# Token-tile start of the first projection, later squares for the second norm, and a PSUM bank for each late half-unit of w_out

## The chip, the cores and the metric

The kernel runs on one core of a Trainium2 chip. The metric is the device time of one launch in microseconds (us). Five engines work side by side, each through its own instruction queue in order: PE (TensorE, matrix products into the eight PSUM banks), DVE (VectorE), ACT (ScalarE), POOL (GpSimd) and SP (SyncE, which issues all the DMAs here). They wait for each other by semaphores alone.

## The reference, cut to what matters

Two layers run over 512 prompt tokens and 64 sample tokens, 576 in all, with a model width of 1024:

```python
for l in range(DEPTH):                       # DEPTH = 2
    xn = rmsnorm(x, norm_mix[l])             # over the 1024 columns of a token
    q, k, v, qi, ki, wi, u, gv = project(xn, w_in[l], pos)
    a = dsa(q, qi, wi, k, v, ki)             # indexer, top-k, attention
    bmix = gelu(u) * spatial(rmsnorm(gelu(gv), gate_norm[l]), w_spatial[l], b_spatial[l])
    x = x + concatenate([a, bmix]) @ w_out[l]
    h = relu(rmsnorm(x, norm_ffn[l]) @ w_ff1[l])
    x = x + (h * h) @ w_ff2[l]               # 1024 -> 4096 -> 1024
y = rmsnorm(x, norm_final)
```

Here `rmsnorm(x, g) = x * rsqrt(mean(x*x) + 1e-6) * g`.

## The kernel before

**Storage.** `x` is kept transposed: 8 column blocks j of 128 features, each over the 576 tokens. Products are made in three parts from float32r pairs: an operand is split into a high part (a rounded copy, made by ACT) and a low part (the rest, made by DVE). `xh` and `xl` are the two parts of x times the norm's gain. The factor 1/rms of a token isn't in them; it is applied later, to a product's result. Weights come in slots of 512 KB: SP loads a slot into one of two raw buffers, ACT writes `ring_hi` (`split_hi`, L631), DVE writes `ring_lo` (`split_lo`, L835), and four such pairs make a ring. A raw buffer is loaded again only when its `split_lo` is done.

**Start of layer 0.** SP issues four small DMAs of norm gains, then x in five token tiles (four of 128 rows and the sample's 64) with two weight slots between them. PE transposes each tile (L1163); ACT copies the blocks into `x` (L650). When all five tiles are there, ACT makes `xh` (L663) and a square (L645) column block by column block, DVE makes `xl` (`feed`, L840), and POOL adds the squares up into `ssacc` (`sum_squares`, L516 and L519). The first projection, QI (index queries), runs weight half by weight half over all tiles: 5 tiles x 2 halves x 12 matmuls of 256 columns (L1179). `row_sums` (L1151) sums `ssacc` over the partitions on PE, `row_mean` and a Newton step make 1/rms. Then PE does the narrow projection of the indexer's keys, `small` (L1373, 32 matmuls), whose weights DVE splits only behind `row_mean`.

**Order.** The rest of a layer up to its feed-forward part runs by ticks: lists written out by hand (`PE_AT`, `ACT_AT`, `DVE_AT`, `POOL_AT`) say what each engine does at each tick of PE's projection and w_out work.

**From w_out to the feed-forward part.** w_out is done in `NWO` = 32 half-units of 12 matmuls with 288 columns (L1211), each a column block j and half of the tokens. The last `KT` = 8, w = 24 to 31, finish blocks 0 to 7. All half-units alternate between banks 0 and 1, and half-unit w waits for the addition of half-unit w-2 (`wo_added`). DVE adds each into `x` (`wo_add`, L1040). When a late one is added, its block is complete, and ACT makes `xh` (L642) and the square (L645) of it, DVE `xl`, POOL adds the square; after every second block a slot of w_ff1 is split. PE's first feed-forward unit, u = 0, waits for all 32 additions and then, block by block, for `xl`. A unit is 48 matmuls of 288 columns into two banks (L1422); there are 64 a layer. Behind u = 1, PE sums `ssacc` into banks 0 and 1 (L1428), from which DVE makes `r2b`, the second norm's factor, used from u = 8 on.

Of the kernel before, what the change touches and what calls it, by code (L numbers as in the profile page):

```python
# [6 lines left out]
def hybrid_encoder_program(nc, A, O):  # L7
# [59 lines left out]
    UNITS = 2 * KT * GROUPS  # L67
    SLOTS = S_FFN + 2 * KT * GROUPS
# [20 lines left out]
    NWO = len(WOUT)  # L89

# [106 lines left out]
    with ctx:  # L197
# [80 lines left out]
        with ExitStack() as area:  # L278
# [3 lines left out]
            early = Area("early", TOK + NT * NSM + ID + P + 2 * NT * NR * 2 * RI + 2 * NT * NIH * ID)  # L282
            small_fm, zs2 = early.take(TOK), early.take(NT, NSM)
            cache_ki, grow = early.take(ID), early.take(P)[0:7 * KT]
            ra, rb = early.take(NT, NR * 2 * RI), early.take(NT, NR * 2 * RI)

            zq = early.take(NT, 2 * NIH * ID)
            early.used -= 2 * NT * NIH * ID
            rl = early.take(2, 2, SEQ)
            early.used = 0  # L290
# [31 lines left out]
        xT_done, xT_evac = sem("xT_done"), sem("xT_evac")  # L322
        gT_done, g_ready = sem("gT_done"), sem("g_ready")
# [28 lines left out]

        FIN_BANKS = [0, 1, 2, 3, 4, 6, 7]
# [29 lines left out]
        def _(sp):  # L383
            row = 0
# [6 lines left out]
            def load_x(t):  # L391
                src = A["x_prompt"][0, t * P:(t + 1) * P, :] if t < NPT else A["x_sample"][0]
                sp.dma_start(x_in[0:ROWS[t], t, :], src).then_inc(x_in_ready[t], 16)

            load_x(0)
            load_x(1)
            for l in range(DEPTH):
# [9 lines left out]
                for c, c0 in enumerate(CHUNKS):  # L407
                    for h in range(2):
                        load(A["w_in"][l, h * KH * P:(h + 1) * KH * P, c0:c0 + CW]
                             .rearrange("(k p) n -> p k n", p=P), KH)  # L410
                        if n[0] == 1:
                            for t in range(2, NT):
                                load_x(t)
# [80 lines left out]
        def _(pool):  # L494
# [13 lines left out]
            g.memset(ssv[:, :], 1.0).then_inc(const_made, 1)  # L508
            link(g.memset(mask0[:, :], 0.0))
# [44 lines left out]
            sum_squares(0)  # L554
            for l in range(DEPTH):
# [52 lines left out]
                for tick in range(G_LAST):  # L608
                    for kind, i in POOL_AT.get(tick, ()):
                        if kind == "gate_newton":  # L610
                            gate_newton(i)
                        elif kind == "gate":
                            gate(i)
                        else:
                            q_rope(i)
                sum_squares(KT * (2 * l + 1))
                sum_squares(KT * (2 * l + 2))
# [6 lines left out]
        def _(act):  # L624
# [8 lines left out]
            def feed(j, stage):  # L633
                base = KT * stage
                if stage % 2:
                    act.wait_ge(wo_added, NWO * (stage // 2 + 1) - KT + j + 1)
                elif stage:
                    act.wait_ge(x_ready, KT * (GROUPS * (stage // 2) - 1) + j + 1)
                else:
                    act.wait_ge(xT_evac, 2 * NT)  # L640
                if 0 < stage < 2 * DEPTH:
                    s.activation(xh[:, j, :], x[:, j, :], ACT.Copy, scale=gain(stage, j)).then_inc(xh_ready, 1)  # L642
                if base + j >= 2:
                    act.wait_ge(ss_added, base + j - 1)
                s.activation(sq[:, j % 2, :], x[:, j, :], ACT.Square).then_inc(sq_ready, 1)  # L645

            for t in range(NT):
                for half in range(2):
                    act.wait_ge(xT_done, 2 * t + half + 1)
                    s.activation(x[:, 4 * half:4 * half + 4, cols(t)],  # L650
                                 bank[2 * (t % 2) + half][:, 0:4 * ROWS[t]].rearrange("p (k n) -> p k n", k=4),
                                 ACT.Copy).then_inc(xT_evac, 1)
                if t == 1:
                    split_hi(0)

            act.wait_ge(g_ready, 1)
            for n in range(NSLOT):
                if n:
                    split_hi(n)
                if n == 0:  # L660
                    act.wait_ge(xT_evac, 2 * NT)
                for j in (2 * n, 2 * n + 1):
                    s.activation(xh[:, j, :], x[:, j, :], ACT.Copy, scale=gain(0, j)).then_inc(xh_ready, 1)  # L663
                for j in (2 * n, 2 * n + 1):
                    feed(j, 0)
            for l in range(DEPTH):
# [131 lines left out]
                for u in range(UNITS):  # L798
                    g, f = divmod(u, 2 * KT)
                    if f < KT:  # L800
# [8 lines left out]
                        s.activation(vh[:, f % KT, :], rl2[:, f % 2, :], ACT.Square).then_inc(h_high, 1)  # L809
                    elif g == GROUPS - 1:  # L810
# [671 lines left out]
```

## Time and profile before

| what | value |
|---|---|
| time, median of 3 runs | 1390.18 us (1389.63 to 1391.34) |
| the profiled execution: its own time | 1390.84 us |
| the profiled execution: span, first to last instruction | 1389.0 us |
| PE busy | 1336.8 us, 96% of the span |
| DVE, ACT, POOL busy | 54%, 37%, 9% |
| DMA | mean 74 GB/s, 16 engines 25% busy |

PE is the engine to read: the other engines idle about half of the time or more, and their idle time alone costs nothing. The places that matter are those at which PE has nothing to do. They show in the view of waits (who waited for whom), in PE's timeline (an entry in square brackets is the idle time ahead of an instruction and what ended it) and in the chain of work that ended last. A busy PE can be slow too: the granted clock tells at which of its two levels, 2.4 or 1.2 GHz (1.00 or 0.50 in the rows), it ran.

### The profile page before, as it was taken

The page shows a single profiled execution, that of the slowest core. Times are in us where ns is not written, and L with a number is a line of the kernel's source. Part 1 is how long each engine was busy: PE and PEld are TensorE (multiplying, and loading weights), DVE is VectorE, ACT ScalarE, POOL GpSimd, SP SyncE. Part 2 cuts the span into 40 slices and gives each one's busy share as a digit, 9 for nine tenths or more (in the row PEclk, how much of TensorE's full clock was granted, in tenths as well). Part 3 has the DMA queues.
Part 4 walks back from the last instruction along what each step waited for, and adds up shares of the span by engine and source line. Part 5 has one row for each costly group of instructions (what it writes and reads, how often), then busy time and mean ns, then how long its engine had stood idle before and what let it go on. Part 6 is the DMA issues. An engine that isn't in the chain of part 4 may idle for free.

```text
span 1389.0 us, 23953 instructions
## 1 busy us (share of the span) xinstructions
PE 1336.8 (96%) x10189; PEld 1318.2 (95%) x10189; DVE 744.7 (54%) x1318; ACT 507.7 (37%) x880; POOL 128.4 (9%) x203
## 2 busy tenths in 40 slices
PE   5999999989999999999999999997999999999997
PEld 4899999989999999999998999997999999999997
DVE  5398965564434344444638987536543444444353
ACT  6463465333123133133336527534321412322322
POOL 4302110210000000000222121003000000000011
PEclk8999999999999999999999999998999999999998
DMA  6123121123232322322321212112323222232311
GB/s 195 32 62 84 32 77 32 32 75 92 77 87 82 85 83 79 89 77 77 96 88 47 75 56 62 31 32 64 89 76 86 82 86 82 77 92 76 86 52 69
DMA packets 169259, 102.48 MB, mean 74 GB/s; under 512 B 6920, under 2 KB 167616, under 8 KB 169152
## 3 DMA queue, kind: packets, MB, share of 16 engines
q1 hardware_dynamic: 169152, 100.94, 25.1%
q8 instruction: 81, 1.33, 0.4%
q14 instruction: 26, 0.21, 0.0%
HBM read 96.98 MB, written 3.95 MB: 73 GB/s over the span
## 4 chain that ended last, share of the span: by engine, by line
PE 85%; DVE 10%; ACT 2%; POOL 1%; issue 1%; DMA 1%; SPq 0%; POOLq 0%; DVEq 0%; ACTq 0%
PE pair L1422 59%; PE pair L1179 8%; PE pair L1211 6%; PE pair L1347 3%; DVE score L934 2%; DVE ring_lo L835 2%; DVE m L932 2%; PE pair L1313 2%; PE pair L1326 1%; DVE xl L840 1%; PE pair L1274 1%; PE pair L1280 1%; PE pair L1255 1%; PE pair L1243 1%; PE pair L1373 1%
## 5 line engine op out<-in xcount | busy, mean ns | idle before, releaser
L631 ACT ACTIVATE ring_hi<-ring_raw 128x1024 fp32r<-128x1024 f32 x176 | 184.5, 1051 | 249.4 <-PE pair L1422 248.7
L835 DVE TENSOR_TENSOR ring_lo<-ring_raw,ring_hi 128x1024 fp32r<-128x1024 f32 x176 | 225.8, 1286 | 40.7 <-ACT ring_hi L631 33.1
L1422 PE MATMUL pair<-xh,ring_hi 128*128 128x288 f32 x1024 | 222.0, 298 | 8.9 <-issue 8.9
L1422 PE MATMUL pair<-xl,ring_hi 128*128 128x288 f32 x1024 | 221.4, 298 | 0.0
L1422 PE MATMUL pair<-xh,ring_lo 128*128 128x288 f32 x1024 | 221.0, 297 | 0.0
L1422 PE MATMUL pair<-vl,ring_hi 128*128 128x288 f32 x1024 | 219.4, 295 | 0.0
L1422 PE MATMUL pair<-vh,ring_hi 128*128 128x288 f32 x1024 | 219.3, 295 | 0.0
L1422 PE MATMUL pair<-vh,ring_lo 128*128 128x288 f32 x1024 | 219.2, 295 | 0.0
L1179 PE MATMUL pair<-ring_hi,xh 128*128 128x256 f32 (+1 forms) x640 | 184.7, 289 | 11.2 <-DVE xl L840 10.2
L1179 PE MATMUL pair<-ring_lo,xh 128*128 128x256 f32 (+1 forms) x640 | 180.6, 282 | 0.0
L1179 PE MATMUL pair<-ring_hi,xl 128*128 128x256 f32 (+1 forms) x640 | 180.6, 282 | 0.0
L1422 PEld LDWEIGHTS pair<-xh,ring_hi 128*128 128x128 f32 x1024 | 167.2, 190 | 9.5 <-issue 9.3
L1105 DVE TENSOR_TENSOR late<-late 128x576 f32<-128x576 f32 x64 | 48.5, 758 | 227.7 <-ACT late L806 227.7
L1422 PEld LDWEIGHTS pair<-xl,ring_hi 128*128 128x128 f32 x1024 | 167.4, 190 | 0.0
L1422 PEld LDWEIGHTS pair<-xh,ring_lo 128*128 128x128 f32 x1024 | 167.3, 190 | 0.0
L1422 PEld LDWEIGHTS pair<-vl,ring_hi 128*128 128x128 f32 x1024 | 165.4, 188 | 0.0
L1422 PEld LDWEIGHTS pair<-vh,ring_lo 128*128 128x128 f32 x1024 | 165.4, 188 | 0.0
L1422 PEld LDWEIGHTS pair<-vh,ring_hi 128*128 128x128 f32 x1024 | 165.2, 188 | 0.0
L1114 DVE TENSOR_TENSOR late<-score,pair 128x288 f32<-128x288 f32 x128 | 52.4, 451 | 200.9 <-PE pair L1422 200.9
L806 ACT ACTIVATE late<-pair 128x288 f32<-128x288 f32 x128 | 45.6, 408 | 272.6 <-PE pair L1422 272.6
L1179 PEld LDWEIGHTS pair<-ring_hi,xh 128*128 128x128 f32 (+1 forms) x640 | 115.4, 180 | 12.7 <-DVE xl L840 10.6
L1179 PEld LDWEIGHTS pair<-ring_lo,xh 128*128 128x128 f32 (+1 forms) x640 | 115.3, 180 | 0.5
(168 smaller groups left out, 1776.8 us busy)
## 6 DMA issues: line engine op xcount, KB each, us to landing
ring_raw<-in_w_ff SPq DMA_DIRECT2D x128, 512.0 KB, 4.0
ring_raw<-in_w_in SPq DMA_DIRECT2D x32, 512.0 KB, 4.1
ring_raw<-in_w_out SPq DMA_DIRECT2D x16, 512.0 KB, 3.5
late<-in_x_prompt SPq DMA_DIRECT2D x4, 512.0 KB, 5.4
out_y_prompt<-late SPq DMA_DIRECT2D x4, 512.0 KB, 2.6
q<-in_w_spatial SPq DMA_DIRECT2D x2, 512.0 KB, 4.3
gate_bc<-in_gate_norm SPq DMA_DIRECT2D x2, 256.0 KB, 5.4
out_k_prompt<-z SPq DMA_DIRECT2D x2, 256.0 KB, 4.5
```

Of the source, the lines that this page charges most:

```text
L631: s.activation(ring_hi[:, n % NSLOT, :], ring_raw[:, n % NRAW, :], ACT.Copy).then_inc(hi_ready, 1)
L806: last = s.activation(rl2[:, f % 2, HALVES[half]], bank[2 * ((u + 1) % 4) + half][:, 0:HALF], ACT.Relu)
L835: v.tensor_tensor(ring_lo[:, n % NSLOT, :], ring_raw[:, n % NRAW, :], ring_hi[:, n % NSLOT, :].bitcast(F32), ALU.subtract).then_inc(lo_rea ...
L932: ins = v.max(m, sc[0:rows, :])
L934: ins = v.match_replace(sc[0:rows, :], m, sc[0:rows, :], TAKEN)
L1105: link(v.tensor_tensor(h32[:, f % 2, :], rl2[:, f % 2, :], rl2[:, f % 2, :], ALU.mult))
L1114: last = v.tensor_tensor(yb[:, j % 2, HALVES[half]], r2b[:, HALVES[half]], bank[b + half][:, 0:HALF], ALU.mult)
L1179: last = mm(out, a[:, kx, cols(t)], b[:, k, :], start=first and k == ks[0] and b is wh and a is xh, stop=final and k == ks[-1] and a is xl)
L1211: last = mm(bank[(NB + w) % 2][:, 0:HALF], b[:, k, :], a[:, KH * h + k, HALVES[half]], start=k == 0 and m == 0, stop=k == KH - 1 and m == 2)
L1313: last = mm(pair[1][0:ROWS[t], e, 0:S], qT[:, a % 2, j, e, 0:ROWS[t]], kTs[:, m, e, :] if t == SMP else kT[:, e, m, 0:S], start=m == 0, st ...
L1347: last = mm(bank[6][0:ROWS[t], h * HD:(h + 1) * HD], pT[0:n, i % 2, e, s * ROWS[t]:(s + 1) * ROWS[t]], vals, start=s == 0, stop=s == nb - 1)
L1422: last = mm(bank[b0 + half][:, 0:HALF], w[:, k, :], a[:, k, HALVES[half]], start=k == 0 and m == 0, stop=k == KT - 1 and m == 2)
```

## The change

The change has three parts, and each can be followed in the code by its names.

- **Start.** The first two tiles of x are issued ahead of the four gain DMAs. PE transposes two tiles, then goes token tile by token tile: QI of tile t, both weight halves, then the transposes of tile t+2. For each tile half DVE multiplies the transposed block by the gain out of PSUM (`x_scale`, into `xg`), ACT makes `xh` from `xg` and copies the raw block into `x` (`x_tile`), DVE makes `xl` (`x_low`). The norm's sum comes from ACT instead of POOL and PE: `x_squares` squares the untransposed rows of `x_in` and accumulates along the row into `ms`, five instructions behind all the tiles and four weight slots.
- **Squares of the second norm.** They leave the `feed` of the w_out stage and stand in the feed-forward units u = 0 to 3, two a unit on ACT. The partition sum goes from behind u = 1 to behind u = `SSB_AT` = 5.
- **Banks.** The late half-units w = 24 to 31 write banks 2, 3, 4, 5, 6, 7, 0, 1, so each waits only for the last earlier use of its own bank. Units u = 0 to 3 wait for the two additions out of their own two banks, not for all.

```diff
+    WO_BANK = [(NB + w) % 2 for w in range(NWO - KT)] + [2, 3, 4, 5, 6, 7, 0, 1]
...
             def feed(j, stage):
-                if 0 < stage < 2 * DEPTH:
+                if stage < 2 * DEPTH:
                     s.activation(xh[:, j, :], x[:, j, :], ACT.Copy, scale=gain(stage, j)).then_inc(xh_ready, 1)
-                if base + j >= 2:
-                    act.wait_ge(ss_added, base + j - 1)
-                s.activation(sq[:, j % 2, :], x[:, j, :], ACT.Square).then_inc(sq_ready, 1)
+                if stage % 2 == 0:
+                    square(base + j)
...
+            def x_tile(t, half):
+                ks = slice(KH * half, KH * half + KH)
+                act.wait_ge(xg_ready, 2 * t + half + 1)
+                s.activation(xh[:, ks, cols(t)], xg[:, t % 2, ks, 0:ROWS[t]], ACT.Copy).then_inc(xs_high, 1)
+                s.activation(x[:, ks, cols(t)], pair[XT_PAIR[t]][:, half, 0:4 * ROWS[t]].rearrange("p (k n) -> p k n", k=4),
+                             ACT.Copy).then_inc(xT_evac, 1)
+            def x_squares(t):
+                act.wait_ge(x_in_ready[t], 16)
+                if t:
+                    act.wait_ge(x_square, t)
+                s.activation(xq[0:ROWS[t], :], x_in[0:ROWS[t], t, :], ACT.Square,
+                             accum_out=ms[0:ROWS[t], t:t + 1]).then_inc(x_square, 1)
+            for t in range(NT):
+                for half in range(2):
+                    x_tile(t, half)
+                if t < 2:
+                    split_hi(t)
+            split_hi(2)
+            split_hi(3)
+            for t in range(NT):
+                x_squares(t)
...
+                        if u < KT // 2:
+                            for j in (2 * u, 2 * u + 1):
+                                square(KT * 2 * l + j)
...
+            for t in range(NT):
+                x_scale(t, 0)
+                x_scale(t, 1)
+                x_low(t, 0)
+                x_low(t, 1)
+                if t < 2:
+                    split_lo(t)
+            split_lo(2)
+            split_lo(3)
...
-                            pe.wait_ge(wo_added, NWO * l + w - 1)
+                        elif WO_BANK[w] in WO_BANK[:w]:
+                            before = max(n for n in range(w) if WO_BANK[n] == WO_BANK[w])
+                            pe.wait_ge(wo_added, NWO * l + before + 1)
...
+                if l == 0:
+                    for t in range(NT):
+                        for h in range(2):
+                            pe.wait_ge(xs_low, 2 * t + h + 1)
+                            index_queries(t, h)
+                        if t + 2 < NT:
+                            x_back(t + 2)
...
-                    elif u == 0:
-                        pe.wait_ge(wo_added, NWO * (l + 1))
+                    else:
+                        pe.wait_ge(wo_added, NWO * (l + 1) - KT + 2 * u + 2)
```

ACT's queue from the last half of the attention output (`vh`) to the first feed-forward unit, before; `late<-x` is the square, `ring_hi` a weight split, `late<-pair` and `vh<-late` the work of u = 0:

```order
L731 ACTIVATE vh<-pair 128x4x128
L642 ACTIVATE xh<-x,gcol 128x576
L645 ACTIVATE late<-x 128x576
L642 ACTIVATE xh<-x,gcol 128x576
L645 ACTIVATE late<-x 128x576
L631 ACTIVATE ring_hi<-ring_raw 128x1024
L642 ACTIVATE xh<-x,gcol 128x576
L645 ACTIVATE late<-x 128x576
L642 ACTIVATE xh<-x,gcol 128x576
L645 ACTIVATE late<-x 128x576
L631 ACTIVATE ring_hi<-ring_raw 128x1024
```

The same place of ACT's queue in the changed kernel, with the first unit's work behind it:

```order
L752 ACTIVATE vh<-pair 128x4x128
L652 ACTIVATE xh<-x,gcol 128x576 x2
L643 ACTIVATE ring_hi<-ring_raw 128x1024
L652 ACTIVATE xh<-x,gcol 128x576 x2
L643 ACTIVATE ring_hi<-ring_raw 128x1024
L652 ACTIVATE xh<-x,gcol 128x576 x2
L643 ACTIVATE ring_hi<-ring_raw 128x1024
L652 ACTIVATE xh<-x,gcol 128x576 x2
L643 ACTIVATE ring_hi<-ring_raw 128x1024
L827 ACTIVATE late<-pair 128x288 x2
L830 ACTIVATE vh<-late 128x576
L660 ACTIVATE late<-x 128x576 x2
```

The eight squares have gone from between the `xh` copies to behind the hidden activations of u = 0 to 3, two each; the splits keep their places.

DVE's queue from the gain copy to the small projection's weights, before:

```order
L853 COPY gcol<-pair 128x56
L835 TENSOR_TENSOR ring_lo<-ring_raw,ring_hi 128x1024
L840 SCALAR_TENSOR_TENSOR xl<-x,gcol,xh 128x576 x2
L835 TENSOR_TENSOR ring_lo<-ring_raw,ring_hi 128x1024
L840 SCALAR_TENSOR_TENSOR xl<-x,gcol,xh 128x576 x2
```

And in the changed kernel, where `early<-pair,gcol` is `x_scale` and `xl<-early,xh` is `x_low`:

```order
L880 COPY gcol<-pair 128x56
L886 TENSOR_TENSOR early<-pair,gcol 128x512 x2
L895 TENSOR_TENSOR xl<-early,xh 128x4x128 x2
L859 TENSOR_TENSOR ring_lo<-ring_raw,ring_hi 128x1024
L886 TENSOR_TENSOR early<-pair,gcol 128x512 x2
L895 TENSOR_TENSOR xl<-early,xh 128x4x128 x2
L859 TENSOR_TENSOR ring_lo<-ring_raw,ring_hi 128x1024
L886 TENSOR_TENSOR early<-pair,gcol 128x512 x2
```

A split of a weight half now stands between the first and the second tile and between the second and the third; four instructions of half a tile each stand where one instruction over a column block stood.

## Rows read from the trace of the kernel before

**Rows 1.** The page: busy us (share of the span) and instructions of PE.

```profile
PE 1336.8 (96%) x10189; PEld 1318.2 (95%) x10189; DVE 744.7 (54%) x1318; ACT 507.7 (37%) x880; POOL 128.4 (9%) x203
```

**Rows 2.** Waits of PE: us in total, times, longest, both layers.

```profile
PE pair L1422 <- issue: 8.9, 2, 4.5
...
PE pair L1211 <- DVE x L1040: 7.3, 4, 2.4
```

**Rows 3.** Timeline of PE, layer 0: start us, us, instruction, [idle before <-releaser].

```profile
269.75 0.29 PE L1211 MATMUL pair<-vh,ring_lo 128*128 128x288 f32 x1
...
280.27 0.29 PE L1211 MATMUL pair<-vh,ring_lo 128*128 128x288 f32 x1
285.02 0.82 PE L1422 MATMUL pair<-xh,ring_hi 128*128 128x288 f32 x2 [4.46 <-issue]
...
293.81 0.42 PE L1422 MATMUL pair<-xh,ring_lo 128*128 128x288 f32 x2
```

**Rows 4.** Timeline of DVE, same stretch.

```profile
264.92 0.82 DVE L840 SCALAR_TENSOR_TENSOR xl<-x,gcol,xh 128x576 fp32r<-128x576 f32 x1 [0.84 <-ACT xh L642]
265.65 0.45 DVE L1040 TENSOR_TENSOR x<-x,pair 128x288 f32<-128x288 f32 x1
...
268.47 1.68 DVE L835 TENSOR_TENSOR ring_lo<-ring_raw,ring_hi 128x1024 fp32r<-128x1024 f32 x1 [0.34 <-ACT ring_hi L631]
270.07 1.95 DVE L840 SCALAR_TENSOR_TENSOR xl<-x,gcol,xh 128x576 fp32r<-128x576 f32 x1
...
285.76 0.82 DVE L840 SCALAR_TENSOR_TENSOR xl<-x,gcol,xh 128x576 fp32r<-128x576 f32 x1 [0.84 <-ACT xh L642]
...
296.68 1.23 DVE L835 TENSOR_TENSOR ring_lo<-ring_raw,ring_hi 128x1024 fp32r<-128x1024 f32 x1
```

**Rows 5.** Timeline of ACT, same stretch.

```profile
264.11 0.78 ACT L642 ACTIVATE xh<-x,gcol 128x576 fp32r<-128x576 f32 x1 [9.47 <-DVE x L1040]
264.79 0.67 ACT L645 ACTIVATE late<-x 128x576 f32<-128x576 f32 x1
...
267.39 1.04 ACT L631 ACTIVATE ring_hi<-ring_raw 128x1024 fp32r<-128x1024 f32 x1
```

**Rows 6.** Timeline of POOL, same stretch: one of the additions of squares.

```profile
267.57 1.50 POOL L519 TENSOR_TENSOR ssacc<-ssacc,late 128x576 f32<-128x576 f32 x1 [1.31 <-ACT late L645]
```

**Rows 7.** Windows: stretch, length, busy us (instructions) by engine, PEclk, DMA share, GB/s.

```profile
285.02:294.23 9.21, 9.21 (x50) 9.21 (x51) 2.48 (x2) 2.23 (x3) 1.48 (x1) 0.69 0.32 92
...
23.00:27.70 4.70, 4.70 (x23) 4.70 (x23) 4.70 (x3) 3.87 (x6) 4.41 (x3) 0.50 0.96 283
```

**Rows 8.** The chain that ended last, in order of time: start us, us, what.

```profile
37.90 4.33 PE pair L1179 x36
42.23 4.22 PE pair L1373 x32
...
301.60 396.79 PE pair L1422 x2976
```

**Rows 9.** Timeline of PE at the start: first transposes, first projection matmul.

```profile
6.04 3.67 PE L1163 MATMUL pair<-ident,late 128*128 128x128 f32 x16 [2.02 <-DMA late<-in_x_prompt]
...
22.65 0.58 PE L1179 MATMUL pair<-ring_hi,xh 128*128 128x256 f32 x1 [8.73 <-DVE xl L840]
```

**Rows 10.** Timeline of SP's queue at the start: first gain, first two x tiles.

```profile
0.72 0.41 SPq L388 DMA_DIRECT2D early<-in_norm_mix  x1
...
2.40 0.89 SPq L393 DMA_DIRECT2D late<-in_x_prompt  x2
```

**Rows 11.** Groups of instructions by line and shape: busy us, mean ns of one, idle before.

```profile
L975 DVE TENSOR_TENSOR early<-pair,gcol 128x512 f32<-128x512 f32 x8 | 5.5, 684 | 6.5 <-PE pair L1274 6.5
...
L697 ACT ACTIVATE q<-late 128x512 f32<-128x512 f32 x8 | 5.0, 624 | 0.1
...
L650 ACT ACTIVATE x<-pair 128x512 f32<-128x512 f32 x8 | 4.6, 596 | 6.4 <-PE pair L1163 6.4
...
L697 ACT ACTIVATION_READ_ACCUMULATOR q<-late 128x1 f32 x8 | 1.5, 190 | 0.0
```

More of the change, by code:

```diff
@@ L647, in _ @@
+            act.wait_ge(g_ready, 1)
             for t in range(NT):
                 for half in range(2):
[L649 to L665, printed above, removed]
+                    x_tile(t, half)
+                if t < 2:
+                    split_hi(t)
@@ L854, in _, with x_scale, x_low @@
             dve.wait_ge(g_ready, 1)
-            for n in range(NSLOT):
-                split_lo(n)
-                feed(2 * n, 0, 0)
-                feed(2 * n + 1, 0, 0)
+            def x_scale(t, half):
+                dve.wait_ge(xT_done, 2 * t + half + 1)
+                ks = slice(KH * half, KH * half + KH)
+                v.tensor_tensor(xg[:, t % 2, ks, 0:ROWS[t]],
+                                pair[XT_PAIR[t]][:, half, 0:4 * ROWS[t]].rearrange("p (k n) -> p k n", k=4),
+                                gcol[:, ks].rearrange("p (k o) -> p k o", o=1).broadcast_to([P, KH, ROWS[t]]), ALU.mult)\
+                    .then_inc(xg_ready, 1)
+            def x_low(t, half):
+                ks = slice(KH * half, KH * half + KH)
+                dve.wait_ge(xg_ready, 2 * t + half + 1)
+                dve.wait_ge(xs_high, 2 * t + half + 1)
+                v.tensor_tensor(xl[:, ks, cols(t)], xg[:, t % 2, ks, 0:ROWS[t]], xh[:, ks, cols(t)].bitcast(F32),
+                                ALU.subtract).then_inc(xs_low, 1)
+            for t in range(NT):
[7 more added lines that the diff above has]
+            split_lo(3)
             for l in range(DEPTH):
@@ L1152, in row_sums, with x_back @@
                 last.then_inc(ss_done, 1)
-            pe.wait_ge(const_made, 5)
+            pe.wait_ge(const_made, 6)
             pe.wait_ge(const_in, 16 * 4)
             tp(bank[7][:, 0:7 * KT], grow[:, :], ident[0:7 * KT, 0:7 * KT]).then_inc(gT_done, 1)
-            for t in range(NT):
+            def x_back(t):
                 pe.wait_ge(x_in_ready[t], 16)
                 for half in range(2):
-                    if t >= 2:
-                        pe.wait_ge(xT_evac, 2 * t + half - 3)
+                    if t == 2:
+                        pe.wait_ge(g_ready, 1)
+                    elif t > 2:
+                        pe.wait_ge(xT_evac, 2 * (t - 2) + half + 1)
+                        pe.wait_ge(xg_ready, 2 * (t - 2) + half + 1)
                     for k in range(4):
-                        last = tp(bank[2 * (t % 2) + half][:, k * ROWS[t]:(k + 1) * ROWS[t]],
+                        last = tp(pair[XT_PAIR[t]][:, half, k * ROWS[t]:(k + 1) * ROWS[t]],
                                   x_in[0:ROWS[t], t, (4 * half + k) * P:(4 * half + k + 1) * P],
@@ L1166, in _ @@
                     last.then_inc(xT_done, 1)
+            x_back(0)
+            x_back(1)
             for l in range(DEPTH):
@@ L1210, in wo_tick @@
                         for m, (b, a) in enumerate(((wh, vh), (wh, vl), (wl, vh))):
-                            last = mm(bank[(NB + w) % 2][:, 0:HALF], b[:, k, :], a[:, KH * h + k, HALVES[half]],
+                            last = mm(bank[WO_BANK[w]][:, 0:HALF], b[:, k, :], a[:, KH * h + k, HALVES[half]],
                                       start=k == 0 and m == 0, stop=k == KH - 1 and m == 2)
```

86 lines of the change are left out of this document (50 added, 36 removed).

## The prediction

> **What bounds the kernel now.** I read the busy times first: PE is busy for 1336.8 of 1389.0 us [rows 1], so no change of order can give more than the 52 us in which PE has nothing to do, plus what it loses at its lower clock. The waits of PE come next. Two of them lie between w_out and the feed-forward part: 7.3 us in four waits for `wo_add` and 8.9 us in two at the first feed-forward unit [rows 2], so 8.1 us a layer. Third, the timeline of that place: the fifth late half-unit (w = 28) ends at 269.75 + 0.29 = 270.04; the eighth ends at 280.56, though three half-units are 3 x 12 matmuls; unit u = 0 starts at 285.02 and ends at 294.23 [rows 3]. Its 48 matmuls took 9.2 us, where 2976 of them took 396.79 us, 0.133 us each [rows 8], so 6.4 us: the granted clock was 0.69 there [rows 7]. What PE waits for is DVE: its queue alternates `wo_add`, `xl` and splits and waits in it for ACT's `xh` [rows 4, 5]. Last, the start: the first projection begins at 22.65, after 8.73 us without work [rows 9], at a granted clock of 0.50 for the next 4.7 us [rows 7], and the small projection ends at 42.23 + 4.22 = 46.45 [rows 8].
>
> **The banks and the moved squares, step by step.** They share one chain, so I cost them together, for layer 0. PE first: with a bank each, w = 29 to 31 follow w = 28 without a wait. A half-unit is 12 x 0.133 = 1.6 us, so they end at 271.6, 273.2 and 274.8.
>
> Now DVE and ACT, which decide when `xl` is ready. Up to the first `xl` (264.92) nothing differs. From there a pair of blocks costs DVE: `wo_add` 0.45, a wait for ACT's `xh` of 0.78 and two handovers of about 0.05, `xl` 0.73 (from its start to the next start, 265.65 - 264.92), the next `wo_add` 0.4, a split, and another `xl` of 0.73, whose `xh` was made beside the split [rows 4, 5]. The split took 1.68 here and the `xl` behind it up to 1.95, while POOL added squares at 1.50 us each [rows 6]; away from POOL the split took 1.23 and `xl` 0.82 [rows 4]. With the squares gone from here POOL is idle, so I take 1.23 and 0.73, and ACT has no 0.67 us square between `xh` and the weight split [rows 5]. The pair is then 0.45 + 0.88 + 0.73 + 0.4 + 1.23 + 0.73, about 4.4; the overlap of an instruction's end with the next one's start takes 0.1 off it: 4.3. The first `xl` of each pair starts at 264.92, 269.2, 273.5, 277.8, and the last one of all ends 2.9 later, at 280.7. Before it ended at 285.76 + 0.82 = 286.6.
>
> PE in unit u = 0 needs one `xl` per 6 matmuls, 0.8 us. Starting at 274.8 it asks for block 7 at 280.4 and gets it at 280.7; the earlier blocks are ahead (block 4 is there at 274.3, block 6 at 278.6). Unit 0 ends at 281.5 instead of 294.2: **12.7 us**. Of these 8.1 are the waits, 2.8 the lower clock, and the rest that unit 0 now runs under DVE's chain instead of behind it. The weights don't come late: the splits for u = 1 to 3 are done at 273.6, 277.9 and 282, their units start at 281.5 or later. Layer 1 has the same waits (two at the first unit and four for `wo_add` in the two layers [rows 2]), so 25.4 in all.
>
> What the squares cost where they go: units 0 to 3 take PE 6.4 us each. ACT's work in one is two hidden activations, a square, a split of 1.04 and now two more squares of 0.67 [rows 5]: below 4 us. DVE's is two instructions of some 0.76 and a split of 1.23 [rows 4], 2.75, and if POOL's two additions of 1.5 [rows 6] held it up for all their length, 5.75. Both stay under 6.4, so the cost is zero; the cover is PE's unit time. The partition sum is 4 matmuls wherever it stands, and `r2b` is wanted at u = 8, two units after u = 5. Cost zero.
>
> **The start.** No row shows this order, so I chain it from its pieces and keep both ends. x is issued first instead of at 2.40 [rows 10], 1.7 us earlier, but PE's queue still has the gain transpose first and the gains now come behind 1 MB of x. PE's transposes began at 6.04 [rows 9]; I take 5.4, between 4.4 (all of the 1.7) and 6.0 (none). Half a tile takes 3.67 / 4 = 0.92 [rows 9], so the first `x_scale` starts at 6.4. It is 0.68 (the same form as L975), each ACT copy of half a tile 0.6 [rows 11], `x_low` taken as 0.68 too. DVE and ACT now hand work to and fro. Tile 0: 0.7, four ACT copies 2.4, `split_hi` 1.04, `split_lo` 1.23 [rows 4, 5]: 11.8. Only then starts tile 1, since `split_lo` stands ahead of its `x_scale`: 0.7 + 2.4 + 1.04 + 1.23, 17.1. PE runs QI of tile 0, half 0, from 11.8, and half 1 only from 17.1, for it needs the second weight half; behind it in PE's queue stand the transposes of tile 2, for which DVE and ACT wait.
>
> From 17.1 PE is the chain. At the lower clock a 256-column matmul took 4.7 / 22 = 0.213 [rows 7], at the full one 4.33 / 36 = 0.12 [rows 8]. Before, the clock stayed low over some 5 us of work from 22.65 on [rows 7, 9]; I take the same from 17.1. Half 1 of tile 0: 2.6; transposes of tile 2: 1.7; QI of tile 1: 3.3, the clock rising in it; transposes 1.0, QI 2.8, the sample's transposes 0.7: 29.2. The sample's `x_scale` and copies bring ACT to 31.0, two splits to 33.1, and then come the five row squares in a line: 1.04 for 1024 columns [rows 5] and 0.19 for the accumulator [rows 11], 6.2 in all: 39.3. The row mean and the split of the small weights follow, 1.0: the small projection starts at 40.3. PE has ended QI at 34.8 and stands idle for 5.5 us, longer than the 4.46 after which unit 0 began at the lower clock [rows 3, 7]; so 21 of the 32 matmuls at 0.24 and 11 at 0.13, 6.6 us, end 46.9. Before it was 46.45. **The start gives nothing, it costs 0.4**: the projection is done 7 us earlier, and the row squares on ACT take its place as what is late. What hangs on the small projection (its copies, the rotation on POOL, the indexer's transposes) is unchanged, so this difference is passed on as it is. The removed `row_sums` (1.0 us of PE) lies inside it.
>
> Sum: -25.4 + 0.4 = -25.0. The profiled execution took 1390.84 (span 1389.0), 0.66 above the median of 1390.18; against the median the forecast is **1365.2**.
>
> **The rivals.**
>
> The start runs cold. PE works there in bursts with waits of 2 to 5 us between them, and after a wait of 8.73 us before it ran at 0.50 [rows 7, 9]. If the clock doesn't rise until the end of the small projection, then QI of tile 1 is 1.8 longer, the later transposes 1.0 and QI of tile 2 2.3 longer, all ahead of ACT's squares (+5.1), and the small projection 1.1: 6.2 more, 1371.4. Against it: from 17.1 on PE has work without a gap. The Trainium skill (TensorE: Matmul & The Clock Gate, section HAM oscillation — how this bites in real kernels) describes a loop whose short bursts alternate with waits, so that every burst starts at the low clock anew; by that rule the time is that of this rival. The rows bear it out for the first matmuls behind a wait, not for an unbroken stretch.
>
> The start gains. If the clock stays at its full level through QI and the small projection, tile 1 and its transposes are 2 us sooner and the small projection 2.4 shorter, of which DVE's and ACT's work behind it lets some 4 through: 1361.2.
>
> DVE's chain doesn't get shorter. If the long split and `xl` of [rows 4] have another cause than POOL, a pair stays at 6.3 us, the last `xl` at 286.6, and unit 0 ends at 287.4: 6.8 a layer instead of 12.7, and 1377.0. The banks then only let PE wait in one place. For it: the causes in rows 4 are inferred. Against it: both are long only where an addition of POOL lies beside them.
>
> Slower than before. The place is units 0 to 3, the mechanism DVE's splits held up by POOL's additions until PE waits for weights. It starts to cost when DVE's work in a unit passes 6.4 us, and eats the 25 us when each of the eight units (two layers) takes 3.1 more, so 9.5 of DVE. At twice the full hold, 2.75 + 2 x 3.0 = 8.8, it would give back 19; at 10 us a unit, 29, and 1394. The longest stretch in the rows, 1.95 for 0.82 [rows 4], would make 6.5 of 2.75. So it is unlikely.
>
> **How the numbers follow.** Forecast 0.64 (1365.2, from 1361 to 1369 with the start's ends and 0.5 a layer), cold start 0.15, gaining start 0.09, DVE's chain unchanged 0.08, slower 0.02; 0.02 are left for no effect at all. A difference of 0.2%, 2.8 us, is about what a measurement of this kernel can tell from none. The range takes in the first three cases and leaves the others out: 1359 to 1374. Faster by more than 0.2%: 0.96; within it: 0.02; slower: 0.02.
>
> **What would show it.** Right: no wait of PE on `wo_add` in w = 29 to 31, unit 0 beginning beside the last three `xl` at a granted clock of 1.00, splits of 1.23 there, POOL idle until unit 0 ends; at the start, a wait of some 5 us ahead of the small projection, ended by DVE behind ACT's row squares, and its end near 47. Wrong: splits still at 1.7 without POOL beside them, waits of PE on `ring_lo` in units 4 to 8, or a granted clock of 0.50 beyond 23 us.

## The result

| kernel | median | runs | ratio to before (95% interval) |
|---|---|---|---|
| before | 1389.91 us | 4 | |
| changed | 1366.71 us (1365.35 to 1367.54) | 4 | 0.983 (0.9814 to 0.9846) |

The change takes 23.2 us off; the forecast was 25.0 (1365.2). The profiled execution took 1367.54 us with a span of 1365.7. Two executions of the experiments below, one of table_early and one of gains_first, ran in a slower state of the chip and are left out of every median and ratio. The page of the profiled execution, first the busy line (as [rows 1]):

```profile
span 1365.7 us, 23949 instructions
...
PE 1327.6 (97%) x10179; PEld 1309.9 (96%) x10179; DVE 733.9 (54%) x1330; ACT 507.6 (37%) x884; POOL 118.8 (9%) x196
```

PE was idle for 52.2 us of the old span, and is for 38.1 now; it is also busy for 9.2 us less with the same matmuls but ten (`row_sums`, about 1 us), so the other part of the gain is in the main work at the higher clock. The waits of PE (us in total, times, longest):

```profile
PE pair L1204 <- DMA early<-in_b_spatial: 6.9, 1, 6.9
PE pair L1233 <- DVE ring_lo L859: 6.1, 2, 4.1
PE pair L1438 <- DVE w_small_r L1093: 4.5, 1, 4.5
...
PE pair L1487 <- DVE xl L864: 0.7, 2, 0.4
```

Both lines of [rows 2] are gone; a wait of 0.4 a layer in the first feed-forward unit (L1487) is what is left of them. The start now has four: for the gains (6.9, where it was 3.7), for the weight halves (`ring_lo`) ahead of tile 0's first half (4.1) and between its two halves (2.06), and ahead of the small projection (L1438). The one of 8.73 for `xl` [rows 9] is gone.

**From w_out to the feed-forward part, layer 0.** DVE (start us, us, instruction, idle before and releaser), as [rows 4]:

```profile
266.95 0.82 DVE L864 SCALAR_TENSOR_TENSOR xl<-x,gcol,xh 128x576 fp32r<-128x576 f32 x1 [0.85 <-ACT xh L652]
...
270.08 1.22 DVE L859 TENSOR_TENSOR ring_lo<-ring_raw,ring_hi 128x1024 fp32r<-128x1024 f32 x1
271.22 0.81 DVE L864 SCALAR_TENSOR_TENSOR xl<-x,gcol,xh 128x576 fp32r<-128x576 f32 x1
...
275.47 0.81 DVE L864 SCALAR_TENSOR_TENSOR xl<-x,gcol,xh 128x576 fp32r<-128x576 f32 x1
...
281.75 0.82 DVE L864 SCALAR_TENSOR_TENSOR xl<-x,gcol,xh 128x576 fp32r<-128x576 f32 x1 [0.85 <-ACT xh L652]
```

A pair of blocks takes 4.27 and 4.25 us (266.95, 271.22, 275.47), where it took 6.3. PE at the end of unit 0, and the stretches ahead of it (windows: stretch, length, busy of PE, PEld, DVE, ACT, POOL, then the granted clock):

```profile
282.62 0.53 PE L1487 MATMUL pair<-xh,ring_hi 128*128 128x288 f32 x2 [0.36 <-DVE xl L864]
...
283.26 0.43 PE L1487 MATMUL pair<-xh,ring_lo 128*128 128x288 f32 x2
```

```profile
266.00:276.90 10.90, 10.90 (x85) 10.90 (x84) 8.11 (x13) 6.01 (x8) 0.00 (x0) 1.00 0.19 52
276.90:283.60 6.70, 6.34 (x48) 6.11 (x47) 5.13 (x7) 4.01 (x5) 0.00 (x0) 1.00 0.52 152
```

PE has no gap in w = 24 to 31, POOL does nothing, and unit 0 runs at the granted clock of 1.00 (2.4 GHz) instead of 0.69 [rows 7]. The unit's last matmuls end at 283.69 (283.26 + 0.43); before, they ended at 294.23 [rows 3].

**The start.** Rows of the chain that ended last (start us, us, what):

```profile
2.99 3.82 DMA early<-in_b_spatial
6.94 0.32 PE pair L1204
7.26 1.06 PE pair L1215 x4
8.42 0.70 DVE early L886
9.20 1.28 ACT L666
10.49 0.63 ACT xh L666
...
13.59 1.22 DVE ring_lo L859
...
18.55 1.24 DVE ring_lo L859
19.92 2.90 PE pair L1233 x12
...
32.62 1.90 ACT ring_hi L643 x2
34.52 1.04 ACT early L674 x2
...
40.94 0.47 DVE w_small_r L1093
41.45 7.04 PE pair L1438 x32
```

The small projection ends at 48.49. Before it ended at 46.45 [rows 8]. So in these two executions the start costs 2.0, and layer 0's unit 0 ends 10.5 earlier: behind the start, 12.6 were gained in this layer.

### The profile page after: what moved, and what is told of

Read it like the earlier page. It is cut to its first block, busy times and chain, and to the rows that moved or that the text cites. A ratio compares the mean times of both kernels' runs of the same rounds, so it can differ in the third digit from the quotient of the medians.

```text
span 1365.7 us, 23949 instructions
## 1 busy us (share of the span) xinstructions
PE 1327.6 (97%) x10179; PEld 1309.9 (96%) x10179; DVE 733.9 (54%) x1330; ACT 507.6 (37%) x884; POOL 118.8 (9%) x196
## 4 chain that ended last, share of the span: by engine, by line
PE 85%; DVE 10%; ACT 2%; POOL 1%; issue 1%; DMA 0%; SPq 0%; POOLq 0%; ACTq 0%; DVEq 0%
PE pair L1487 59%; PE pair L1233 9%; PE pair L1266 6%; PE pair L1402 3%; DVE score L982 2%; DVE m L980 2%; PE pair L1368 2%; DVE ring_lo L859 2%; PE pair L1381 2%; PE pair L1329 1%; DVE xl L864 1%; PE pair L1438 1%; PE pair L1335 1%; PE pair L1310 1%; PE pair L1298 1%; ACT xh L652 1%
## 5 line engine op out<-in xcount | busy, mean ns | idle before, releaser
L859 DVE TENSOR_TENSOR ring_lo<-ring_raw,ring_hi 128x1024 fp32r<-128x1024 f32 x176 | 220.5, 1257 | 39.8 <-ACT ring_hi L643 33.1
L1487 PE MATMUL pair<-xh,ring_hi 128*128 128x288 f32 x1024 | 219.9, 296 | 0.7 <-DVE xl L864 0.7
L1487 PE MATMUL pair<-vl,ring_hi 128*128 128x288 f32 x1024 | 219.3, 295 | 0.0
L1487 PE MATMUL pair<-xh,ring_lo 128*128 128x288 f32 x1024 | 219.3, 295 | 0.0
L1487 PE MATMUL pair<-vh,ring_lo 128*128 128x288 f32 x1024 | 219.3, 295 | 0.0
L1487 PE MATMUL pair<-xl,ring_hi 128*128 128x288 f32 x1024 | 219.3, 295 | 0.0
L1487 PE MATMUL pair<-vh,ring_hi 128*128 128x288 f32 x1024 | 219.3, 295 | 0.0
L1487 PEld LDWEIGHTS pair<-xh,ring_hi 128*128 128x128 f32 x1024 | 165.3, 188 | 1.4 <-DVE xl L864 1.2
L1487 PEld LDWEIGHTS pair<-xh,ring_lo 128*128 128x128 f32 x1024 | 165.3, 188 | 0.0
L1487 PEld LDWEIGHTS pair<-vh,ring_lo 128*128 128x128 f32 x1024 | 165.3, 188 | 0.0
L1487 PEld LDWEIGHTS pair<-vl,ring_hi 128*128 128x128 f32 x1024 | 165.3, 188 | 0.0
L1487 PEld LDWEIGHTS pair<-vh,ring_hi 128*128 128x128 f32 x1024 | 165.2, 188 | 0.0
L1487 PEld LDWEIGHTS pair<-xl,ring_hi 128*128 128x128 f32 x1024 | 165.2, 188 | 0.0
```

Source lines behind the costliest of these rows:

```text
L859: v.tensor_tensor(ring_lo[:, n % NSLOT, :], ring_raw[:, n % NRAW, :], ring_hi[:, n % NSLOT, :].bitcast(F32), ALU.subtract).then_inc(lo_rea ...
L1487: last = mm(bank[b0 + half][:, 0:HALF], w[:, k, :], a[:, k, HALVES[half]], start=k == 0 and m == 0, stop=k == KT - 1 and m == 2)
```

## The experiments

Eleven kernels were run, in three sessions, each beside its own runs of the kernel before (medians 1389.29, 1388.74 and 1389.72). Where two kernels of different sessions are compared, the ratios are the fairer measure; each has about 2 us to either side.

| kernel | what differs | median | ratio (95%) |
|---|---|---|---|
| old_start | before + banks + moved squares | 1364.17 | 0.9821 (0.9806 to 0.9836) |
| new_start | before + new start | 1391.36 | 1.0015 (1.0006 to 1.0025) |
| banks_alone | before + banks | 1380.16 | 0.9933 (0.9916 to 0.9949) |
| squares_alone | before + moved squares | 1375.85 | 0.9904 (0.9889 to 0.9919) |
| banks_no_adds | banks, squares in place, their additions cut | 1367.78 | 0.9846 (0.9831 to 0.9860) |
| table_early | changed + an early activation | 1365.19 | 0.9824 (0.9807 to 0.9840) |
| gains_first | changed, gains issued ahead of x | 1366.71 | 0.9835 (0.9815 to 0.9855) |
| row_squares_early | changed, row squares early | 1358.83 | 0.9782 (0.9767 to 0.9797) |
| rows_table | row_squares_early + table_early | 1357.24 | 0.9763 (0.9747 to 0.9779) |
| rows_scale | row_squares_early, tile 1's `x_scale` early | 1356.00 | 0.9753 (0.9738 to 0.9768) |
| rows_all | all of the last four edits | 1353.61 | 0.9739 (0.9723 to 0.9755) |

### Which part gave the time: old_start and new_start

The first keeps the kernel before and takes only the banks and the later squares:

```diff
+    WO_BANK = [(NB + w) % 2 for w in range(NWO - KT)] + [2, 3, 4, 5, 6, 7, 0, 1]
...
-                s.activation(sq[:, j % 2, :], x[:, j, :], ACT.Square).then_inc(sq_ready, 1)
+                if stage % 2 == 0:
+                    square(base + j)
...
+                        if u < KT // 2:
+                            for j in (2 * u, 2 * u + 1):
+                                square(KT * (2 * l + 1) + j)
```

> The kernel before with the banks and the moved squares, and the old start. My theory: the whole gain lies between w_out and the first feed-forward unit, 12.6 us a layer, and the new start costs 2.0. So 1389.9 - 25.3 = 1364.6 us, 2 us under the changed kernel (1366.7). Rival: the start brings part of the gain (its projection ends earlier); then this kernel is slower than the changed one, 1368 or more.

The second takes the changed kernel and puts banks and squares back:

```diff
-    WO_BANK = [(NB + w) % 2 for w in range(NWO - KT)] + [2, 3, 4, 5, 6, 7, 0, 1]
+    WO_BANK = [(NB + w) % 2 for w in range(NWO - KT)] + [(NB + w) % 2 for w in range(NWO - KT, NWO)]
...
-    SSB_AT = 5
+    SSB_AT = 1
...
-                if stage % 2 == 0:
-                    square(base + j)
+                square(base + j)
```

> The changed kernel with the old banks, the squares back in the w_out stage and the partition sum behind u = 1: the new start alone. My theory: 1389.9 + 2.0 = 1391.9 us. Rival (the start gains): under 1389.

Measured: 1364.17, 25.1 below before, and 1391.36, 2.1 above it. The two add up to -23.0 where the changed kernel has -23.2. So the whole gain lies at the feed-forward entry, and the new start alone makes the kernel slower, by 0.15% with an interval from 0.06 to 0.25%.

### Banks and squares apart: banks_alone, squares_alone, banks_no_adds

banks_alone is old_start without the moved squares: the table of banks and the waits that follow it.

```diff
+    WO_BANK = [(NB + w) % 2 for w in range(NWO - KT)] + [2, 3, 4, 5, 6, 7, 0, 1]
...
-                    elif u == 0:
-                        pe.wait_ge(wo_added, NWO * (l + 1))
+                    else:
+                        pe.wait_ge(wo_added, NWO * (l + 1) - KT + 2 * u + 2)
```

> The kernel before with a bank for each late half-unit and the two-additions wait, squares where they were. My theory: DVE's chain stays at 6.3 us a pair, its last xl at 286.6, unit 0 ends at 287.4 instead of 294.2: 6.8 a layer, 1376.3 us; if PE's clock falls in the gaps of unit 0, up to 1382. Rival (the wait for the banks was all there was): 1364.6.

squares_alone is old_start without those: the squares in units 0 to 3, the partition sum behind u = 5.

```diff
+    SSB_AT = 5
...
-                s.activation(sq[:, j % 2, :], x[:, j, :], ACT.Square).then_inc(sq_ready, 1)
+                if stage % 2 == 0:
+                    square(base + j)
```

> The kernel before with the squares moved to units 0 to 3 and the partition sum behind u = 5, banks and waits as before. My theory: DVE's pair falls to 4.3 us, so half-units wait for additions only 1 us in all and end at 276.2, but unit 0 waits for all additions (278.9) and ends at 285.3: 8.9 a layer, 1372 us; if the clock falls in the 2.7 us ahead of unit 0, up to 1378. Rival (squares hidden before, only the banks count): 1389.9.

Alone they give 9.1 and 13.4, together 25.1. That is 2.6 more than their sum, which intervals of about 2 us on each of the three don't settle. DVE's queue in banks_alone shows what the squares do (same columns as above), and POOL's what stands beside it:

```profile
271.00 1.68 DVE L836 TENSOR_TENSOR ring_lo<-ring_raw,ring_hi 128x1024 fp32r<-128x1024 f32 x1 [0.34 <-ACT ring_hi L632]
272.61 1.98 DVE L841 SCALAR_TENSOR_TENSOR xl<-x,gcol,xh 128x576 fp32r<-128x576 f32 x1
```

```profile
270.10 1.50 POOL L520 TENSOR_TENSOR ssacc<-ssacc,late 128x576 f32<-128x576 f32 x1 [1.31 <-ACT late L646]
272.29 1.69 POOL L520 TENSOR_TENSOR ssacc<-ssacc,late 128x576 f32<-128x576 f32 x1 [0.69 <-ACT late L646]
```

The pair of blocks stays at 6.3 us there (272.61, then 278.94), the long split and the long `xl` are still there, and PE's waits have moved to unit 0. The granted clock is 0.50 (1.2 GHz) in the stretch from 285 to 290, behind the longest of them:

```profile
PE pair L1424 <- DVE xl L841: 9.3, 8, 3.2
```

```profile
285.00:290.00 5.00, 2.52 (x9) 2.18 (x10) 3.46 (x5) 2.29 (x3) 2.56 (x2) 0.50 0.37 105
```

In squares_alone DVE is at its short pair (splits 1.22, a pair 4.26), but all additions still come before unit 0, so PE stands idle ahead of it:

```profile
277.90 0.50 PE L1430 MATMUL pair<-xh,ring_hi 128*128 128x288 f32 x2 [2.44 <-issue]
```

Whether POOL is the cause of the long splits was only inferred in the prediction. banks_no_adds keeps ACT's squares in the w_out stage and POOL's additions in number, but cuts seven of eight additions to one column:

```diff
-                        ins = g.tensor_tensor(ssacc[:, 0:TOK], ssacc[:, 0:TOK], sq[:, j % 2, :], ALU.add)
+                        wide = TOK if base % (2 * KT) == 0 else 1
+                        ins = g.tensor_tensor(ssacc[:, 0:wide], ssacc[:, 0:wide], sq[:, j % 2, 0:wide], ALU.add)
```

> As banks_alone, but POOL adds only one column of seven of the eight squares of the second norm instead of 576 (the sum of squares is left out, so the second norm is wrong); ACT's squares stay in their place. It tells POOL's part of the long splits from ACT's. My theory: the splits fall from 1.68 to 1.22 and the xl behind them from 1.95 to 0.82, ACT's square leaves a wait of 0.34 a pair: 4.6 us a pair, last xl at 281.7, unit 0 ends at 282.5: 11.7 a layer, 1366.5 us. Rival (the long splits have another cause, such as ACT's square or a transfer beside them): the same as banks_alone, 1376 or more.

```profile
268.98 1.23 DVE L837 TENSOR_TENSOR ring_lo<-ring_raw,ring_hi 128x1024 fp32r<-128x1024 f32 x1 [0.34 <-ACT ring_hi L633]
270.12 0.81 DVE L842 SCALAR_TENSOR_TENSOR xl<-x,gcol,xh 128x576 fp32r<-128x576 f32 x1
```

The split is 1.23 and `xl` 0.81 with nothing else changed on DVE; the pair is 4.69 (265.43 to 270.12). The 0.34 that DVE waits for ACT's split is the square still in ACT's queue, and the 0.42 between 4.69 and 4.27 is about that. The time, 1367.78, is 12.4 below banks_alone and 3.6 above old_start (by the ratios 12.1 and 3.5). So POOL's additions are the cause of the long instructions, and of the 16.0 that the squares cost beside the banks they are 12.4.

The sizes fit a hold to the end of POOL's instruction. In banks_alone the split began with 0.60 of POOL's addition to go (271.60 - 271.00) and took 0.46 more than 1.22; `xl` began with 1.37 to go (273.98 - 272.61) and took 1.16 more than 0.82. The Trainium skill (SBUF — State Buffer, section Who interferes with whom) says that a DVE instruction with two SBUF inputs contends with a GpSimd instruction that reads SBUF, and that what they contend for is an exclusive lock; these two agree, but for 0.14 and 0.21 us at the end of POOL's. POOL is held in turn: in banks_no_adds its one-column addition takes 0.24 at 268.08, and 0.72 at 270.26, where it begins beside the `xl` that ends at 270.93.

### What the new start pays for: row_squares_early, table_early, gains_first

Three places of the start were late in the changed kernel's chain: the five row squares on ACT (34.52 to 40.5), ACT's table load (9.20), and the gains that land behind x (2.99 to 6.81). Each was moved by itself.

```diff
                 if t < 2:
                     split_hi(t)
+                if t == 1:
+                    for n in range(NT):
+                        x_squares(n)
             split_hi(2)
             split_hi(3)
-            for t in range(NT):
-                x_squares(t)
```

> The changed kernel with ACT's five row squares moved from behind the fourth weight split to behind the second one, into the 5.8 us in which ACT waits for PE's transposes of tile 2. My theory: the small projection no longer waits for them (4.5 us) and starts at 37 without a gap, so PE keeps its full clock and takes 4.2 instead of 7.0 us for it: 7 us less, 1359.7 us. Rival (PE's order of the projection is the limit and the clock stays low): 4.5 us or less, 1362 or more.

Measured 1358.83. ACT now does the row squares in the time in which it waited for the transposes of tile 2, and the small projection follows QI without a wait, at its full pace (chain of row_squares_early):

```profile
32.25 5.83 PE pair L1234 x48
38.08 4.23 PE pair L1439 x32
```

It ends at 42.31 instead of 48.49, 6.2 earlier: 4.5 of wait in the profile before, and 2.8 because its 32 matmuls took 4.23 instead of 7.04, less the 1.1 by which QI ended later in this execution (38.1 for 36.9), at the lower pace for longer. Of the medians' 7.9 below the changed kernel (6.7 by the ratios) these 6.2 are what the two profiles show. In the changed kernel the granted clock was 0.50 in it (1.2 GHz) behind that wait (windows, columns as above):

```profile
42.00:44.00 2.00, 2.00 (x10) 1.77 (x10) 0.00 (x0) 0.84 (x3) 0.78 (x4) 0.50 0.00 0
```

This run beats both kernels.

```diff
+            act.wait_ge(const_made, 6)
+            s.activation(xq[:, 0:1], ones[:, 0:1], ACT.Copy)
             act.wait_ge(g_ready, 1)
```

> The changed kernel with one activation of a single column ahead of ACT's first wait, so that the load of ACT's function table (1.28 us, at 9.20 in the changed kernel, at 0.72 in the kernel before) no longer stands behind the first x_scale. My theory: the whole chain up to the small projection starts 1.28 us earlier, 1365.4 us. Rival (what PE waits for hides it): 1366.7.

Measured 1365.19; by its ratio it can't be told from the changed kernel, and its trace isn't read here.

```diff
-            load_x(0)
-            load_x(1)
             row = 0
...
                 row += v.shape[0]
+            load_x(0)
+            load_x(1)
```

> The changed kernel with the four DMAs of the gains issued ahead of the first two x tiles, as before. My theory: the gains land at 3.7 instead of 6.9, so PE's transposes begin when x lands, 6.0 to 6.3 instead of 7.2: 1.0 us less, 1365.7 us. Rival (x is what PE waits for, so issuing it first is worth 1.7 us): 1367 to 1368.

Measured 1366.71, nothing gained. PE's timeline shows that the edit did what it should at its own place: the gain transpose at 3.75, the first transposes at 6.08 (7.19 in the changed kernel).

```profile
3.75 0.32 PE L1204 MATMUL pair<-ident,early 56*128 56x56 f32 x1 [3.75 <-DMA early<-in_b_spatial]
6.08 3.29 PE L1215 MATMUL pair<-ident,late 128*128 128x128 f32 x16 [2.01 <-DMA late<-in_x_prompt]
```

In that profile the small projection begins at 40.51 and takes 7.09, so 0.9 of the 1.1 had reached it; the median doesn't show it, and its interval (2.8 us to either side) couldn't. What the two edits are worth alone stays open; the next runs put them on a start without the row squares.

### The rest of the chain: rows_table, rows_scale, rows_all

> The changed kernel with two edits together: the five row squares behind the second weight split on ACT, and a one-column activation ahead of the first real one, so that ACT's table load (1.28 us, begun at 9.07 in the trace with the early row squares alone) lies in ACT's idle time. The row squares alone gave 1358.83. Theory: with the row squares out of the way the start is one chain through DVE, ACT and PE up to tile 1's split_lo, then PE, so the table load is on it whole: 1.28 off, 1357.5. Rival: the chain that counts begins with PE's transposes of tile 2 or ends with DVE's splits, and the load is covered: 1358.8.

Measured 1357.24, 1.6 below row_squares_early (2.6 by the ratios, with 3 to either side, so the times alone don't tell it from nothing). In the profile the load stands at 0.72, under the wait for x, and the small projection ends at 40.46 (36.24 + 4.22), 1.85 earlier. The second half of tile 0 begins 1.1 earlier (18.71 for 19.79), though the gains landed 0.2 later in this execution; so the load was on the chain for about its whole 1.28. The rest of the 1.85 is PE's pace: it rose right behind the transposes of tile 2 here, and 8 matmuls later in row_squares_early.

```profile
18.71 0.55 PE L1236 MATMUL pair<-ring_hi,xh 128*128 128x256 f32 x1 [2.06 <-DVE ring_lo L862]
...
23.22 0.28 PE L1236 MATMUL pair<-ring_lo,xh 128*128 128x256 f32 x1
23.34 0.28 PE L1236 MATMUL pair<-ring_hi,xl 128*128 128x256 f32 x1
```

rows_scale adds this on DVE:

```diff
             for t in range(NT):
-                x_scale(t, 0)
-                x_scale(t, 1)
+                if t != 1:
+                    x_scale(t, 0)
+                    x_scale(t, 1)
                 x_low(t, 0)
                 x_low(t, 1)
+                if t == 0:
+                    x_scale(1, 0)
+                    x_scale(1, 1)
                 if t < 2:
                     split_lo(t)
```

> The changed kernel with the early row squares, and on DVE the two x_scale of tile 1 ahead of the first split_lo. In the trace with the early row squares alone, DVE waits 0.67 for split_hi ahead of split_lo(0) (13.46) and the two x_scale of tile 1 take 1.28 behind it; ACT idles 1.89 in between. Theory: the x_scale fill that wait, tile 1's xh begin about 1.9 sooner, right behind split_hi(0), and its split_lo ends some 1.2 to 1.9 sooner; split_lo(0) ends 0.6 later, but PE, which then has QI of tile 0's first half, isn't late by it for long: 1358.83 - 1.3 = 1357.5. Rival: PE's second half follows its first only with the clock still low, so what is gained is idle time ahead of it and nothing at the end: 1358.8.

Measured 1356.00, and in the profile the small projection ends at 38.07 (33.63 + 4.44): 4.2 earlier than in row_squares_early, where the theory had 1.3. PE's timelines say why. In row_squares_early the second half of tile 0 has to wait, and the matmuls behind it start every 0.21 us, up to 25.87:

```profile
19.79 0.55 PE L1234 MATMUL pair<-ring_hi,xh 128*128 128x256 f32 x1 [2.06 <-DVE ring_lo L860]
...
24.41 0.41 PE L1234 MATMUL pair<-ring_lo,xh 128*128 128x256 f32 x1
24.62 0.41 PE L1234 MATMUL pair<-ring_hi,xl 128*128 128x256 f32 x1
...
25.87 0.28 PE L1234 MATMUL pair<-ring_hi,xl 128*128 128x256 f32 x1
25.98 0.28 PE L1234 MATMUL pair<-ring_hi,xh 128*128 128x256 f32 x1
```

In rows_scale the two halves follow each other, and from the second on they start every 0.12:

```profile
17.79 0.41 PE L1238 MATMUL pair<-ring_hi,xl 128*128 128x256 f32 x1
18.00 0.38 PE L1238 MATMUL pair<-ring_hi,xh 128*128 128x256 f32 x1
18.22 0.28 PE L1238 MATMUL pair<-ring_lo,xh 128*128 128x256 f32 x1
18.34 0.28 PE L1238 MATMUL pair<-ring_hi,xl 128*128 128x256 f32 x1
```

So behind the wait of 2.06 PE kept the lower pace for 20 matmuls and the 8 transposes of tile 2. How long it keeps it differs between executions with the same wait: in the changed kernel and in rows_table the pace rose right behind the transposes, 8 matmuls sooner, so about 1 of the 4.2 is row_squares_early's late rise and not the edit's. The Trainium skill (TensorE: Matmul & The Clock Gate, section HAM oscillation — how this bites in real kernels) describes short bursts with longer waits between them, each burst starting at the low clock anew; the trace agrees for the burst behind the wait, though the burst ahead of it hadn't reached the full pace either. One pair of profiles shows it; the medians (2.8 apart, by the ratios 4, with 3 to either side) agree in sign and don't settle the size.

> The changed kernel with the early row squares, the one-column activation, tile 1's x_scale ahead of the first split_lo, and the gain DMAs issued ahead of x. Theory: each takes its time off the one chain of the start (row squares 7.9, table load 1.28, x_scale 1.3, gains 0.7 to 1.1): 1366.71 - 7.9 - 1.28 - 1.3 - 0.7 = 1355.5. Rival: below the row squares something else sets the end (the clock's rise, or POOL's and ACT's work behind the row mean), and the three together give less than 1: 1358.

Measured 1353.61, the fastest kernel here: 13.1 below the changed one. The small projection ends at 35.74 (31.29 + 4.45). The expectation was passed by 1.9; the `x_scale` edit had been worth more than the sum allowed it. There is time left in this start: in rows_scale and rows_all the chain that ended last runs through the five row squares again, since they now hold up ACT's `xh` of tile 2 (22.44 in rows_scale, where DVE waits 1.73 for it).

## Why the prediction was right, step by step

**PE in w = 29 to 31** follows without a wait: right.

**DVE's pair**, forecast 4.3 instead of 6.3: 4.27 and 4.25. The `xl` of the last block ended 15.8 after the first one's start by the forecast, and 15.6 (282.57 - 266.95) in the trace. Two of the numbers that the sum was made of, the split at 1.23 and the `xl` at its short form, hold because POOL is idle; banks_no_adds shows that this was the cause, and banks_alone what the rival "DVE's chain doesn't get shorter" would have given: the rival put the banks alone at 13.6, and they gave 9.1. It had PE's waits in unit 0 in its sum, but not the granted clock of 0.50 behind them; in banks_alone ten matmuls behind the last wait took 2.5 us (289.28 to 291.81) instead of 1.3, and eighteen in layer 1 took 4.3 (956.63 to 960.96) instead of 2.4. That is 3.1 of the 4.5 between the two; the rest stays open.

**Unit 0**, forecast 12.7 a layer: it ends 10.5 earlier by the clock of the span, and the `xl` of the first block came 2.03 later (266.95 for 264.92), so 12.6. Doubled that is 25.1, and old_start measured 25.1. One part of the forecast's 12.7 was read wrongly, though the sum holds. Beside 8.1 of waits and 2.8 of lower clock it gave the rest to unit 0 running under DVE's chain instead of behind it, but that is what takes away the wait of 4.46, and is counted with the waits. The rest was lower clock too, ahead of unit 0: between two waits for `wo_add` PE did w = 29 and 30 in 5.1 us (272.44 to 277.52 in the kernel before), and their 24 matmuls at 0.133 are 3.2.

```profile
274.00:276.00 2.00, 2.00 (x9) 1.82 (x9) 1.66 (x3) 1.96 (x3) 1.33 (x1) 0.50 0.00 0
```

**The squares in units 0 to 3 for nothing**: right. PE waits 0.7 in all of L1487, for `xl` in unit 0, and never there for a weight half. POOL's additions did lengthen DVE's work once a layer, and it stayed under PE's unit time (layer 0):

```profile
287.28 1.94 DVE L859 TENSOR_TENSOR ring_lo<-ring_raw,ring_hi 128x1024 fp32r<-128x1024 f32 x1 [1.26 <-ACT ring_hi L643]
...
293.69 1.22 DVE L859 TENSOR_TENSOR ring_lo<-ring_raw,ring_hi 128x1024 fp32r<-128x1024 f32 x1 [1.27 <-ACT ring_hi L643]
```

**The start**, forecast +0.4: the mechanism was right and the term too small; it is 2.0 in the profiles and 2.1 in the medians of new_start. That the row squares on ACT are late next was the forecast, with a wait of 5.5 ahead of the small projection; it is 4.5, and moving them gives 7.9 (6.7 by the ratios). Its working went off in four places:

- PE's first transposes were put at 5.4, between 4.4 and 6.0. They began at 7.19. The bound was wrong because it held the landing of the gains at its old place; the last of the four is issued at 2.99 behind 1 MB of x and lands 3.82 later. Issued ahead of x, it was there at 3.75. That is 1.8.
- ACT's table load, 1.28, wasn't in the sum. It stood at 0.72 under the wait for x in the kernel before; ACT's first activation now stands behind two waits (`g_ready`, then `xg_ready`), and the load began only when both were met. So QI begins at 14.96 instead of 11.8.
- ACT's steps are shorter than I took them: it starts its copies about every 0.5, where 0.6 each was in the sum. With that and a clock that rose earlier in QI than forecast (matmuls start every 0.12 from 24.06), ACT begins its row squares 1.4 later than the forecast's 33.1 instead of 3.
- The small projection was put at 6.6, and took 7.04: more of its matmuls ran at the lower level.

Together the small projection ended 1.6 later than the forecast's 46.9. That it is so little is in part luck: the first two steps alone made QI 3.2 late, and the third, an error the other way, took more than half of that back. The lower pace lasted to 23.9, a little beyond the 23 us that the forecast named as a sign of being wrong (the small projection, for which it had the lower clock in its sum, aside); splits of 1.7 without POOL and waits for `ring_lo` in units 4 to 8, its other two signs, did not show.

**The rivals.** "The start runs cold" went one step its way: the wait between the two halves of tile 0 kept PE at the lower pace, as rows_scale shows, but from tile 1 on work was unbroken and the pace rose. Its 1371.4 was not reached. "The start gains" (1361.2) had the wrong road: the clock alone doesn't do it while the row squares are late, and with them moved the kernel is at 1358.8. "Slower" found no place.

## What to carry to other kernels

When work is brought forward so that its input comes sooner, look at what was put at its tail to make room: here the tail (five squares) cost what the head had gained, though ACT had idle time of the same length earlier in its queue. An engine that adds for a side result can hold the one on the path: move it to where the path is another engine's. And parts that share one chain are costed as one chain, since each alone leaves a wait that the other takes away: 9.3 us in unit 0 with the banks alone, 4.9 ahead of it with the squares alone, 0.7 with both.

## What the runs showed of the hardware that was not expected

- A small transfer issued behind two large ones on SP's queue landed 3.82 us after its issue (2.99 to 6.81); with the small ones first, the last was there at 3.75.
- ACT's table load (1.28 us) can lie on the path or off it. In the kernel before it ran at 0.72, though the activation that it belongs to began at 7.19; in rows_table too it ran at 0.72, ahead of an activation at 2.14. Both activations stand behind one wait. In the changed kernel the first one stands behind two, and the load ran at 9.20, behind both. That the number of waits decides is not shown.
- At the start the granted clock in the windows doesn't always go with the pace: in the changed kernel the stretch below shows 1.00 while matmuls of 256 columns start every 0.21 us, and in rows_scale a stretch with the same pace shows 0.50. There I went by the pace, and "lower pace" above means 0.21 us a matmul and not a reading of the granted clock.

```profile
20.00:22.50 2.50, 2.50 (x12) 2.50 (x13) 0.00 (x0) 0.00 (x0) 0.00 (x0) 1.00 0.60 163
```

```profile
15.30:17.90 2.60, 2.60 (x12) 2.60 (x12) 2.29 (x3) 2.51 (x5) 0.00 (x0) 0.50 0.62 147
```
